# Seven block products in place of eight in three feed-forward blocks

## The reference, cut to what matters

```python
def swiglu(h, w_in, w_out):
    gate, up = jnp.split(h @ w_in, 2, axis=-1)
    return (jax.nn.silu(gate) * up) @ w_out
...
x = x + 0.5 * swiglu(rms_norm(x, ffn_norm[l, 0]), ffn_w_in[l, 0], ffn_w_out[l, 0])
```

## Time and profile before

| What | Value |
|---|---|
| median of three runs | 2168.82 us |
| the profiled execution, its own time | 2161.44 us |
| its span | 2159.4 us |
| PE busy | 1912.5 us (89%) |
| DVE busy | 1319.4 us (61%) |
| ACT busy | 809.6 us (37%) |
| POOL busy | 604.0 us (28%) |
| granted TensorE clock, mean | 0.975 |
| HBM traffic, mean | 236 GB/s |

### The profile page before, as it was taken

The page is one execution under the profiler, slowest core; times in us unless marked ns, Lnnn a source line. Parts: engine busy times, 40 slices in busy tenths (PEclk is TensorE's granted clock), DMA queues, the critical chain, the costliest instruction groups (busy, mean ns, idle before and its releaser), DMA issues.

```text
span 2159.4 us, 30419 instructions
## 1 busy us (share of the span) xinstructions
PE 1912.5 (89%) x11687; PEld 1397.2 (65%) x11687; DVE 1319.4 (61%) x2197; ACT 809.6 (37%) x1285; POOL 604.0 (28%) x650
## 2 busy tenths in 40 slices
PE   7999777887776677678999999999999999989999
PEld 4997753443222222224888888988887788778887
DVE  4877695665656666645554757455456654586444
ACT  3336231322212112112444555335435444475443
POOL 1000266666667666665000001323000000021000
PEclk9999999999999999999999999999999999989999
DMA  9983499999999999997755321035555555415553
GB/s 353 359 271 98 161 349 382 364 354 371 356 367 376 348 378 369 357 379 294 241 192 189 120 90 52 5 114 181 186 183 175 177 193 187 163 59 176 190 182 115
DMA packets 251470, 510.35 MB, mean 236 GB/s; under 512 B 14810, under 2 KB 165036, under 8 KB 248284
## 3 DMA queue, kind: packets, MB, share of 16 engines
q0 software_dynamic: 74416, 270.83, 33.2%
q1 hardware_dynamic: 173802, 233.95, 32.9%
q10 hardware_dynamic: 3138, 4.00, 0.6%
HBM read 507.68 MB, written 1.05 MB: 236 GB/s over the span
## 4 chain that ended last, share of the span: by engine, by line
PE 60%; POOL 12%; DVE 8%; issue 8%; DMA 7%; ACT 3%; another core or an unknown queue 2%; ACTq 0%; SPq 0%; DVEq 0%; POOLq 0%
PE bank_pair L760 21%; PE bank_pair L794 11%; PE bank_pair L443 9%; POOL big L1978 7%; PE bank_pair L1850 5%; DMA big<-in_peer_v,aux 2%; POOL hf L1978 2%; POOL aux L1978 2%; PE bank_pair L3225 2%; PE bank_pair L2720 1%; DMA big<-in_peer_u,aux 1%; DMA big<-in_w_mod 1%; DVE big L2096 1%; DVE w_lo L354 1%
## 5 line engine op out<-in xcount | busy, mean ns | idle before, releaser
L354 DVE TENSOR_TENSOR w_lo<-w_raw,w_hi 128x2048 fp32r<-128x2048 f32 x196 | 449.1, 2292 | 257.8 <-ACT w_hi L349 257.4
L349 ACT ACTIVATE w_hi<-w_raw 128x2048 fp32r<-128x2048 f32 x196 | 374.5, 1912 | 216.4 <-PE bank_pair L760 107.4
L1850 PE MATMUL bank_pair<-big 128*128 128x512 f32 x676 | 337.8, 627 | 110.1 <-DMA big<-in_peer_v,aux 72.9
L1850 PEld LDWEIGHTS bank_pair<-big 128*128 128x128 f32 x676 | 119.6, 194 | 307.6 <-DMA big<-in_peer_v,aux 167.7
L760 PE MATMUL bank_pair<-w_hi,hh 128*128 128x512 f32 x704 | 277.5, 396 | 3.1 <-DVE x L1654 1.7
L2096 DVE SCALAR_TENSOR_TENSOR big<-big,bank_pair 128x1024 f32<-128x1024 f32 x172 | 208.8, 1217 | 114.9 <-DMA big<-in_peer_u,aux 97.8
L760 PE MATMUL bank_pair<-w_lo,hh 128*128 128x512 f32 x704 | 273.1, 390 | 0.0
L760 PE MATMUL bank_pair<-w_hi,hl 128*128 128x512 f32 x704 | 265.6, 390 | 0.2 <-DVE hl L695 0.2
L1978 POOL DMA_INDIRECT big<-in_peer_v,aux x172 | 165.7, 963 | 104.7 <-issue 45.9
L1978 POOL DMA_INDIRECT big<-in_peer_u,aux x172 | 164.0, 954 | 72.7 <-issue 47.9
L1963 ACT ACTIVATE big<-ident,aux 128x128 f32<-128x128 f32 x252 | 84.3, 390 | 259.1 <-issue 91.9
(11 more groups left out here) (516 smaller groups left out, 3285.6 us busy)
## 6 DMA issues: line engine op xcount, KB each, us to landing
w_raw<-in_ffn_w_in SPq DMA_DIRECT2D x176, 512.0 KB, 4.6
w_raw<-in_ffn_w_out SPq DMA_DIRECT2D x44, 1024.0 KB, 4.9
big<-in_w_mod SPq DMA_DIRECT2D x24, 1024.0 KB, 8.1
w_raw<-in_w_in SPq DMA_DIRECT2D x22, 1024.0 KB, 9.6
w_raw<-in_rwkv_w_rkv SPq DMA_DIRECT2D x12, 1024.0 KB, 5.6
w_raw<-in_peer_w_query SPq DMA_DIRECT2D x8, 1024.0 KB, 5.9
w_raw<-in_w_kv SPq DMA_DIRECT2D x8, 1024.0 KB, 5.2
w_raw<-in_w_out SPq DMA_DIRECT2D x4, 1024.0 KB, 5.3
```

The lines of the kernel that those rows point to most:

```text
L349: act.activation(to, w_raw[i][:, :], ACT.Copy).then_inc(S("w_hi"), 1)
L354: dve.tensor_tensor(lo, w_raw[i][:, :], hi.bitcast(F32), ALU.subtract).then_inc(S("w_lo"), 1)
L1850: mm = pe.matmul(bank[4 + 2 * tt + half][:, :], diag[:, r % VDIAGS, :], ring_rows[turn % RROWS][:, half * 512:(half + 1) * 512], start=(r ...
```

## The change

In the blocks 0, 1 and 3 (`WIDE_FFNS`) the tiles 2 and 3, 5 and 6, 8 and 9 are made in pairs ("S"); tiles 0, 1, 4, 7 and 10 stay as they are ("R"). For a pair, the 2 x 2 blocks of tokens (two groups of 128 tokens by two halves of the input rows) meet the 2 x 2 blocks of weights (two halves of the rows by 512 gate and 512 up columns). The eight block products are replaced by seven of 12 matmuls each, on sums and differences of blocks: the scheme of Strassen in Winograd's form. A block in which this is done has 42 slots in place of 33. One round of a pair and the ordinary tile after it is the slots b11, t1, t2, o, t3, b21, t4, b22, g0, g1, o, o, where o is a down slot.

What is new beside the products:

- SP loads seven blocks' worth of weights for a pair in five plain DMAs of 1 MB with rows of 2 KB, into buffers of their own (`wide_raw`), and POOL adds two further blocks onto two of them by an accumulating DMA from HBM (`wide_pool`). DVE makes two further sums (`wide_sum`), each as long as a split.
- Once in each block, ACT scales the tokens (8 activations of 128 x 256), DVE makes four sums and differences of 128 x 512 (`token_sums`), ACT rounds them, and DVE writes their low part (`token_rest`).
- For each pair DVE combines products in five operations of 128 x 512 (`partial`), ACT copies one bank (`gate_copy`), and silu, multiplication, rounding and rest are done at 128 x 512 (`wide_silu_out`, `wide_mult`, `wide_round`, `wide_rest`).
- SP's list is written out, with the first pair's loads among those of tiles 0 and 1.

```diff
+WIDE_FFNS = (0, 1, 3)
...
+FFN_UNITS = {f: [("R", i) for i in range(FTILES)] if f not in WIDE_FFNS else
+             [("R", 0), ("R", 1), ("S", 2), ("R", 4), ("S", 5), ("R", 7), ("S", 8), ("R", 10)] for f in range(4)}
...
+        def wide_pool(pool, f, tiles):
+            for tile in tiles:
+                for step in ("t1", "t3"):
+                    wide_landed(pool, step, f, tile)
+                    pool.dma_start(wide_raw[step].rearrange("p (k c) -> p k c", k=4),
+                                   wide_block(f, tile, *WIDE_ADDED[step]), accum_op=ALU.add)                        .then_inc(S(f"{step}_added"), 16)
...
+                def wide(block, i):
+                    if i == 2:
+                        sp.wait_ge(S("slot_done"), base + (f == 0))
+                    else:
+                        sp.wait_ge(S("w_lo"), SLOT[f, "t4" if block == "b11" else block, i - 3] + 1)
...
+                ring("g0", 1)
+                wide("t1", 2)
+                ring("g1", 1)
+                wide("b11", 2)
+                wide("b22", 2)
+                ring("o", 0)
+                wide("t3", 2)
+                wide("b21", 2)
+                for i in (2, 5, 8):
+                    ring("o", i - 1)
+                    ring("g0", i + 2)
+                    ring("g1", i + 2)
+                    if i < 8:
+                        wide("t1", i + 3)
+                        wide("t3", i + 3)
+                    ring("o", i)
+                    if i < 8:
+                        ring("o", i + 1)
+                        wide("b11", i + 3)
+                        wide("b22", i + 3)
+                        wide("b21", i + 3)
...
+            def block(tile, step, b, a_hi, a_lo, start, stop):
+                n = SLOT[f, step, tile]
+                pe.wait_ge(S("w_lo"), n + 1)
+                wh, wl = (w[n % WRING][:, :].rearrange("p (k c) -> p k c", k=4) for w in (w_hi, w_lo))
+                for k in range(4):
+                    for m, (a, w) in enumerate(((a_hi, wh), (a_hi, wl), (a_lo, wh))):
+                        mm = pe.matmul(bank[b][:, :], a[:, k, :], w[:, k, :], start=(start and k == 0 and m == 0),
...
             silu(0, base, 0)
             hi.upto(base + 4)
+            if f in WIDE_FFNS:
+                for k in range(KT):
+                    a = act.activation(fm(token_flat)[:, k, :], xf[:, k, :], ACT.Copy, scale=col(GAIN[norm], k))
+                a.then_inc(S("token_sum_hi"), 1)
+                act.wait_ge(S("token_sum_hi"), EARLIER["token_sum_hi"] + 3 * WIDE_FFNS.index(f) + 2)
+                act.activation(over_big[4][:, :], bigs(5), ACT.Copy).then_inc(S("token_sum_hi"), 1)
             act_round(0, 0)
...
+            def token_sums():
+                o(dve.tensor_tensor(first, a21, a22, ALU.subtract))
+                o(dve.tensor_tensor(third, a11, a21, ALU.subtract))
+                o.wait()
+                o(dve.tensor_tensor(second, first, a11, ALU.subtract))
+                o.wait()
+                o(dve.tensor_tensor(fourth, a12, second, ALU.add))
+                o.wait()
+                dve.sem_inc(S("token_sum_hi"), 1)
...
+            if f in WIDE_FFNS:
+                token_sums()
             act_rest(0, 0)
+            if f in WIDE_FFNS:
+                lo.upto(base + 5)
+                token_rest()
+                mult(1, 2)
+                wide_sum("t2", 2)
+                lo.upto(base + 6)
+                for tile in (2, 5, 8):
...
+                lo.upto(at + 11)
+                mult(FTILES - 1, (0, 2))
+                lo.upto(base + FFN_COUNT[f] - 1)
+                act_rest(FTILES - 1, 2, True)
...
             if f == 3:
+                hi.upto(base + FFN_COUNT[f] - 1)
                 residual_out(0)
...
             act.activation(last_hi, bank[2][:, :], ACT.Copy).then_inc(S("ffn_act_hi"), 1)
             if f == 3:
                 residual_out(3)
-            hi.upto(base + 34)
+            hi.upto(base + FFN_COUNT[f] + 1)
```

More of the change, by code:

```diff
@@ new lines, in of_tokens, with of_sums, wide_products, summed @@
+            def of_tokens(tt, half):
+                return [a[:, 4 * half:4 * half + 4, tt * P:(tt + 1) * P] for a in (hh, hl)]
+            def of_sums(i):
+                return token_hi[:, i, :, :], token_lo[:, i, :, :]
+            def wide_products(tile):
+                w = wide_number(f, tile)
+                def summed(count):
+                    pe.wait_ge(S("ffn_sum"), EARLIER["ffn_sum"] + 5 * w + count)
+                block(tile, "b11", 0, *of_tokens(0, 0), True, False)
+                pe.wait_ge(S("token_sum"), EARLIER["token_sum"] + WIDE_FFNS.index(f) + 1)
+                block(tile, "t1", 3, *of_sums(0), True, False)
+                block(tile, "t2", 1, *of_sums(1), True, False)
+                n = SLOT[f, "o", tile - 1]
+                down_wait(n, tile - 1)
+                for part in range(4):
+                    mm = down(n, n % WRING, False, False, part)
+                mm.then_inc(S("slot_done"), 1)
+                summed(1)
+                block(tile, "t3", 1, *of_sums(2), False, False)
+                pe.wait_ge(S("gate_copy"), EARLIER["gate_copy"] + w + 1)
+                block(tile, "b21", 0, *of_tokens(0, 1), False, True)
+                summed(2)
+                block(tile, "t4", 1, *of_tokens(1, 1), False, True)
+                summed(3)
+                block(tile, "b22", 3, *of_sums(3), False, True)
@@ new lines, in token_rest, with wide_sum @@
+            def token_rest():
+                dve.wait_ge(S("token_sum_hi"), EARLIER["token_sum_hi"] + 3 * WIDE_FFNS.index(f) + 3)
+                dve.tensor_tensor(over_big[7][:, :], bigs(5), over_big[4][:, :].bitcast(F32), ALU.subtract)\
+                   .then_inc(S("token_sum"), 1)
+            def wide_sum(step, tile):
+                if step == "t2":
+                    wide_added(dve, "t1", f, tile)
+                    wide_landed(dve, "b22", f, tile)
+                    dve.wait_ge(S("w_lo"), SLOT[f, "b11", tile] + 1)
+                    first, second = "t1", "b22"
+                else:
+                    wide_landed(dve, "b21", f, tile)
+                    wide_summed(dve, "t2", f, tile)
+                    dve.wait_ge(S("w_lo"), SLOT[f, "t2", tile] + 1)
+                    first, second = "t2", "b21"
+                dve.tensor_tensor(wide_raw[step], wide_raw[first], wide_raw[second], ALU.add)                   .then_inc(S("wide_sum"), 1)
@@ new lines, in partial @@
+            def partial(tile, count):
+                home, part, b, step = ((wide_up[0], wide_silu[1], 1, "t2"), (wide_up[1], wide_silu[1], 1, "t3"),
+                                       (wide_up[1], wide_up[1], 3, "t3"), (wide_silu[1], wide_silu[1], 1, "t4"),
+                                       (wide_up[0], wide_up[0], 3, "b22"))[count - 1]
+                dve.wait_ge(S("slot_done"), SLOT[f, step, tile] + 1)
+                before = EARLIER["ffn_sum"] + 5 * wide_number(f, tile)
+                if count == 1:
+                    dve.wait_ge(S("gate_copy"), EARLIER["gate_copy"] + wide_number(f, tile) + 1)
+                if count in (3, 4):
+                    dve.wait_ge(S("ffn_sum"), before + count - 1)
+                dve.tensor_tensor(home, bank[b][:, :], part, ALU.subtract if b == 3 else ALU.add).then_inc(S("ffn_sum"), 1)
```

296 lines of the change are left out of this document (244 added, 52 removed).

## The result

The changed kernel takes 2198.69 us as the median of five runs (2197.25 to 2203.53); the kernel before, beside it on the same chip, 2168.82 us (2166.10 to 2172.77). The ratio is 1.0149 [1.0130, 1.0169], so the change makes the kernel 28 to 37 us slower. The forecast was +29.2 us and 2198 us.

What follows compares the result with a forecast made beforehand. PE was taken to bound the blocks. -24.5 + 21.4 + 7.3 + 7.3 + 3 x 2.7 + 2 x 2.8 + 4 = +29.2 us, 2168.8 + 29.2 = 2198 us; eight in ten, 2176 to 2232.

Steps and rivals of the forecast that it cites:

- Taken away, 24.5 us: Inside the blocks: 84 gate/up matmuls a pair instead of 96 save 2.72 us a pair, 24.5 us in nine.
- The other engines keep up: Inside the blocks: of a 47.8 us round DVE needs 40 and ACT 27.5, DMA load 93%; PE sets the pace.
- Rival 1: Inside rounds: adds cost three copies or more, the DMA queue sets the pace, 28 us more, 2226 us; 18%.
- The start of block 0, 21.4 us: Before slot 4 of block 0: PE waits 21.4 us for late weights and the token chain behind them.
- The start of blocks 1 and 3, 7.3 each: Before slot 4 there: PE waits 7.3 us each for slot 4's weights, then an 11.3 us chain.
- Rival 2: Queue keeps up at block starts: waits 4.1 us (blocks 1, 3), 18 (block 0), full clock; 2184 us, 17%.
- Rivals 3 and 4: Waits before slot 4 sum below 11 us, faster, 2158 or 2144 us, 8%; sum to 11 us, no change, 5%.
- Behind slot 4, 2.7 us in each block: After slot 4 in blocks 0, 1 and 3: two PE waits, 1.3 and 1.4 us, on DVE's list.
- The clock, 4 us: After the long waits before slot 4: PE at 1.2 GHz costs 2 + 1 + 1 = 4 us, from 0 to 8.
- The ends, 5.6 us: End of blocks 0 and 1: PE waits 2.8 us each because the last down slot is rounded late.

Runs made afterwards that it cites:

- three mends: Changed kernel with g1 and slot 4's weights loaded before t1, tokens scaled and summed before slot 2, last down slot rounded early: 2149.67 us, ratio 0.9951.
- all four: Changed kernel with slot 4's weights first, tokens earlier, last down rounding earlier, and block 0's small loads behind the first pair's adds: 2077.75 us, ratio 0.9913.
- the first experiment: Changed kernel with g1 and slot 4's weights issued on SP ahead of t1 and b11 in blocks 0, 1 and 3: 2170.33 us, ratio 1.0050.
- the one edit: Changed kernel with ACT rounding the last down slot before the last activation's rounding in blocks 0 and 1 too: 2183.10 us, ratio 1.0113.

## Why the prediction was right

The accounts of the kernels, in us. Pairs are taken at -2.55 each. "Other waits" are those at a block's start and the 0.69 at the end of block 3, and "ends" those before the last down slot. The half clock is what slot 4 took over the 5.44 us of the earlier trace rows, then what the last down slot took over its count behind the wait at a block's end, then what block products took behind waits of their own. Measured is the share by which the ratio differs from 1, times 2168.82:

| Kernel | pairs | waits before slot 4 | other waits | ends | half clock | sum | measured |
|---|---|---|---|---|---|---|---|
| the change | -23 | 35.5 | 2.5 | 5.5 | 7.1 + 3.4 | +31 | +32 [28, 37] |
| slot 4's weights first | -23 | 12.1 | 4.4 | 5.5 | 6.6 + 1.7 + 1.7 | +9 | +11 [7, 15] |
| tokens earlier | -23 | 16.6 | 4.4 | 5.5 | 2.0 + 3.4 | +9 | +10 [7, 14] |
| last rounding earlier | -23 | 34.5 | 3.2 | 0 | 7.3 + 0 | +22 | +25 [20, 29] |
| adds as copies | -23 | 35.8 | 3.0 | 5.5 | 6.5 + 1.5 | +29 | +38 [33, 42] |
| block 0 without pairs | -15.3 | 10.4 | 2.1 | 2.8 | 3.2 + 0 | +3 | +6 [3, 10] |
| three mends | -23 | 0 | 11.1 | 0 | 0 + 0 + 1.5 | -10 | -11 [-14, -7] |
| small loads late | -23 | 27.5 | 3.2 | 5.5 | 7.6 + 1.7 | +22 | +22 [12, 33] |
| all four | -23 | 0 | 7.2 | 0 | 0 + 0 + 2.5 | -13 | -19 [-26, -12] |

The second term of the half clock is read behind the wait that ends block 1 in the changed kernel:

```profile
1672.40 0.63 PE L934 MATMUL bank_pair<-w_lo,hh 128*128 128x512 f32 x1
...
1674.96 0.63 PE L934 MATMUL bank_pair<-w_lo,hh 128*128 128x512 f32 x1
```

Six steps of 0.427 us lie between these two, 0.2 more each than at full clock, and with the steps at both ends it is 1.7 us; block 0 shows the same. The sums explain the order of the kernels and nearly their distances. Seven of the nine lie within about 3 us of what was measured, and the last one within its wide interval. The adds as copies do not fit: they measure 8 us more than their sum, outside their interval. Their profiled execution (2188.64 us) was 6 us below their median, so most of that is in executions without a trace, and it stays open.

By the steps of the forecast:

- **Taken away, 24.5 us.** Right, 23 measured by rounds, 2.6 us a pair where nothing else is late.
- **The other engines keep up.** Right: no wait over 0.15 us in any round of the changed kernel but the 0.37 in block 3 at its start, with DVE 80% busy. Rival 1, adds of three copies, is out: the share is 0.85, an add is two copies.
- **The start of block 0, 21.4 us.** 1.48 + 21.61 = 23.1 measured. From the first matmul of slot 0 the weights were there after 35.6 us (33.5 forecast), and the chain behind them took 11.24 (11.3).
- **The start of blocks 1 and 3, 7.3 each.** 6.65 and 7.21. In block 1 landing came 18.4 us after slot 0's start (18.9 forecast) and the chain took 11.25. Rival 2, a queue quick enough, would have shown 4.1: nearly that appears in all three blocks when slot 4's weights go first, and once, in block 1, with the order left alone (3.85, in the kernel without pairs in block 0). So the 2.8 us that the late landing adds in block 1 are not there in every execution. Rivals 3 and 4 needed the three waits to stay at or below 11 us in sum; they were 35.5.
- **Behind slot 4, 2.7 us in each block.** Wrong: only 0.37 us in block 3, nothing above 0.15 in the others. The step took slot 4 to last 5.4 us. At half clock it lasted 8.29, 8.03 and 7.05, and DVE used that time. The kernels with slot 4 of block 1 at 7.06 to 7.12 us show a wait of 0.94 to 1.01 us behind it, the changed kernel with 8.03 none, which fits the same reading. So do the others with the tokens in their old place: wherever slot 4 took 7.9 us or more there is no such wait (but the 3.35 us of the first experiment, which hangs on a load), and at 7.0 to 7.7 us there is one of 0.34 to 1.01. An estimate from block 1, 1.6 us of slow slot and 1.0 of wait, gives 2.6, near the forecast; block 3 gives 1.6 + 0.4 = 2.0.
- **The clock, 4 us.** Too small: slot 4 took 2.9 + 2.6 + 1.6 = 7.1 us more, and the two slots behind the end waits 3.4, which the forecast did not count at all. The term of the clock was mis-sized by 6.5 us, that of the waits behind slot 4 by 7.7 the other way, and they come in good part from the same event: 4 + 8.1 = 12.1 forecast, 10.5 + 0.4 = 10.9 measured. The forecast did not foresee that one takes the place of the other; that its sum came out so close is in this part luck.
- **The ends, 5.6 us.** 2 x 2.74 measured, gone with the one edit.

So the mechanism is shown by undoing its parts: moving the weights' place in the queue, the tokens, the small loads or the last rounding each takes away the wait, or the part of it, that was put down to it. The sign was decided by them, not by the arithmetic saved. What was only argued is that the slow slot 4 is why no wait follows it; no run held the clock up to test it.

## What to carry to other kernels

Saving one in eight of a pair's gate and up matmuls pays 2.6 us a pair only where PE is already the bound, while the new setup work is paid in full where PE has nothing else to do; so place setup by the landing it will hang behind, not by the slot it is needed in. Of the loads that one engine issues in a row, put the one that is needed first at the head even if another buffer is free earlier, and look for small loads of another queue that share the same engines. A wait's releaser names only the last link: follow the chain one or two steps back, then test by moving one link at a time, since here two causes stand behind one wait: of the 6.65 us in block 1, moving the loads alone leaves 4.35, moving the tokens alone 0.59.

## What the runs showed of the hardware that was not expected

PE's clock fell behind waits of only 3.9 us too, and behind 7 of the 11 waits of 2.74 or 2.76 us at the ends of blocks 0 and 1 in all kernels. The first matmuls behind the wait, in the changed kernel:

```profile
1066.22 0.63 PE L934 MATMUL bank_pair<-w_lo,act_hi 128*128 128x512 f32 x1
1066.65 0.63 PE L934 MATMUL bank_pair<-w_hi,act_lo 128*128 128x512 f32 x1
```

They start 0.43 us apart, at 1.2 GHz, against 0.227 before. Behind the wait of 3.87 us in the first experiment slot 4 took 7.96 us, behind 21.61 us 8.29: a wait five times as long cost scarcely more clock. The Trainium skill's "TensorE: Matmul & The Clock Gate", section "Part 1: The HAM clock gate (the "warmup" mystery)", says that the array runs at half speed after an idle time, and the trace agrees. And a slow stretch on PE isn't wholly lost: the engines that were next to be late caught up in it, which is, by the rows above but without a run that holds the clock up, why the waits forecast behind slot 4 did not appear.

An accumulating DMA from HBM cost two copies of DMA time (2.9 us more for 1 MB), and also more of POOL's time to issue: 1.27 to 1.45 us, against 0.75 to 0.84 for the plain copies of the same blocks.
